# Gate products of a product-key expert layer from bf16 one-hots, the gate in three parts, the masks with four tokens innermost

## What is computed

```python
def block(xb):                       # 128 tokens
    q = (xb @ w_pq).reshape(PEER_BLOCK, P_HEADS, 2, P_HALF)
    sc = jnp.einsum('thpc,hpkc->thpk', q, sub_keys)
    sv, si = lax.top_k(sc, TOPK)
    cand = (sv[..., 0, :, None] + sv[..., 1, None, :])...     # 16 x 16 sums
    cid = (si[..., 0, :, None] * N_KEYS + si[..., 1, None, :])...
    fv, fi = lax.top_k(cand, TOPK)
    eid = jnp.take_along_axis(cid, fi, axis=-1)
    g = jax.nn.softmax(fv.astype(jnp.float32), axis=-1).astype(xb.dtype)
    ue = jnp.take(u_experts, eid, axis=0)
    ve = jnp.take(v_experts, eid, axis=0)
    a = jax.nn.gelu(jnp.einsum('thkd,td->thk', ue, xb), approximate=False)
    return jnp.einsum('thk,thkd->td', g * a, ve)
```

## Time and profile before

| | us |
|---|---|
| median of 3 runs (2201.74 to 2204.07) | 2202.97 |
| the profiled execution | 2208.66 |
| its span (first to last instruction) | 2207.0 |

### The profile page before, as it was taken

One profiled execution on the slowest core, in us unless ns is written; L12 is line 12 of the kernel. 1 busy time (PEld: TensorE's weight loads), 2 busy tenths in 40 slices (PEclk: granted clock), 3 DMA queues, 4 the chain that ended last, 5 costly groups with the idle time before them and its releaser, 6 DMA issues. The chain is left out here.

```text
span 2207.0 us, 46403 instructions
## 1 busy us (share of the span) xinstructions
PE 2152.3 (98%) x14712; PEld 2005.6 (91%) x14712; DVE 1683.5 (76%) x2461; ACT 1098.2 (50%) x1651; POOL 367.5 (17%) x344
## 2 busy tenths in 40 slices
PE   6999999999999999999989999999999999999998
PEld 6999899999999988888889989999999998888886
DVE  6665658999999687677775746599999996667776
ACT  6445454444444454554464545444444445554454
POOL 3110110000000155334230101100000002333442
PEclk9999999999999999999998999999999999999999
DMA  5444466765555677777644444567655557777774
GB/s 192 153 144 152 145 207 213 230 203 178 173 174 176 224 260 242 239 242 243 223 135 135 150 166 168 188 225 231 194 175 176 171 176 256 244 240 242 241 240 164
DMA packets 173982, 437.49 MB, mean 198 GB/s; under 512 B 19360, under 2 KB 84896, under 8 KB 172752
## 3 DMA queue, kind: packets, MB, share of 16 engines
q1 hardware_dynamic: 173232, 432.09, 59.5%
q0 software_dynamic: 672, 4.39, 0.6%
HBM read 399.70 MB, written 36.70 MB: 198 GB/s over the span
## 5 line engine op out<-in xcount | busy, mean ns | idle before, releaser
L746 DVE TENSOR_TENSOR w_lo<-raw,w_hi 128x1024 fp32r<-128x1024 f32 x680 | 844.7, 1245 | 401.8 <-ACT w_hi L714 183.1
L1143 PE MATMUL ps<-act_hi,w_hi 128*128 128x256 f32 x2880 | 829.6, 288 | 3.2 <-DVE act_lo L797 1.9
L1143 PE MATMUL ps<-act_lo,w_hi 128*128 128x256 f32 x2880 | 819.8, 285 | 0.0
L1143 PE MATMUL ps<-act_hi,w_lo 128*128 128x256 f32 x2880 | 819.8, 285 | 0.0
L1143 PEld LDWEIGHTS ps<-act_hi,w_hi 128*128 128x128 f32 x2880 | 558.1, 194 | 5.5 <-DVE act_lo L797 2.3
L1143 PEld LDWEIGHTS ps<-act_hi,w_lo 128*128 128x128 f32 x2880 | 558.2, 194 | 0.1
L1143 PEld LDWEIGHTS ps<-act_lo,w_hi 128*128 128x128 f32 x2880 | 557.5, 194 | 0.0
L714 ACT ACTIVATE w_hi<-raw 128x1024 fp32r<-128x1024 f32 x248 | 263.1, 1061 | 323.5 <-PE ps L1403 311.7
L1403 PE MATMUL ps<-w_hi,act_hi 128*128 128x512 f32 x1000 | 389.2, 389 | 2.0 <-DVE act_lo L1107 2.0
L1403 PE MATMUL ps<-w_lo,act_hi 128*128 128x512 f32 x1000 | 389.0, 389 | 0.0
L1403 PE MATMUL ps<-w_hi,act_lo 128*128 128x512 f32 x1000 | 389.0, 389 | 0.0
(11 more groups left out here) (248 smaller groups left out, 2105.9 us busy)
## 6 DMA issues: line engine op xcount, KB each, us to landing
raw<-slabs SPq DMA_DIRECT2D x684, 512.0 KB, 3.6
h_park<-h_out SPq DMA_DIRECT2D x256, 128.0 KB, 1.7
h_in<-h_park SPq DMA_DIRECT2D x250, 128.0 KB, 3.7
memT<-mem POOLq DMA_DIRECT2D x2, 1024.0 KB, 6.6
skT<-sub_keys POOLq DMA_DIRECT2D x2, 1024.0 KB, 8.0
x_park<-xT SPq DMA_DIRECT2D x2, 1024.0 KB, 5.4
xT<-x_park SPq DMA_DIRECT2D x2, 1024.0 KB, 8.4
xT<-x SPq DMA_DIRECT2D x1, 1024.0 KB, 5.0
```

The lines of the kernel that those rows point to most:

```text
L746: nc.vector.tensor_tensor(w_lo[:, j].rearrange("p k c -> p (k c)"), raw[:, j, :], w_hi[:, j].rearrange("p k c -> p (k c)").bitcast(FP32), ...
L1143: last = nc.tensor.matmul(ps[:, j, 0:T], w[:, j, k, :], a[:, k, :], start=(k == 0 and i == 0), stop=(k == KB - 1 and i == 2))
```

## The change

`iota`, `row_is` and the picks become bf16 (keys up to 127 are exact in it). `iota` and `row_is` get four tokens as their innermost dimension: `iota` holds each number four times in a row. `rowT`, `colT` and `gate2` become one tile `picks` with five rows: row key, column key, and the gate in three bf16 parts (rounded part, rounded rest, rest of the rest; `g_rest` is float32). `hot_row` becomes bf16, three parts, four tokens innermost; `hot_col` becomes bf16, still token by token in memory, but written through a view with the token innermost. The gate product has three matmuls a token for two, each reading `hot_row` with a step of four elements.

```diff
+PARTS = 3
-        hot_col = at("hot_col", x_at, [P, 4, P], F32R)
-        hot_row = at("hot_row", x_at + 2048, [P, 2, 4, P], F32R)
+        hot_col = at("hot_col", x_at, [P, 4, P], BF16)
+        hot_row = at("hot_row", x_at + 2048, [P, PARTS, P, 4], BF16)
-        iota = sb("iota", [P, P])
+        iota = at("iota", top[0], [P, P, 4], BF16)
-        row_is = at("row_is", par_at, [P, 4, P], BF16)
+        row_is = at("row_is", par_at, [P, P, 4], BF16)
-        rowT = sb("rowT", [P, T])
-        colT = sb("colT", [P, T])
-        gate2 = sb("gate2", [P, 2, T], F32R)
+        picks = at("picks", top[0], [P, 2 + PARTS, T], BF16)
+        g_rest = tmp("g_rest", 104, [P, T])
-            nc.gpsimd.iota(iota[:], [[1, P]], base=0, channel_multiplier=0,
+            nc.gpsimd.iota(iota[:], [[1, P], [0, 4]], base=0, channel_multiplier=0,
-                                                        (b_f, iota, ALU.is_equal, cols, col_f)):
+                                                        (b_f, iota[:, :, 0], ALU.is_equal, cols, col_f)):
-                step.mark(nc.vector.tensor_copy(rowT[:], ps[:, 4, 0:T]))
-                step.mark(nc.vector.tensor_copy(colT[:], ps[:, 4, T:2 * T]))
-                step.link(nc.vector.tensor_copy(gate2[:, 0], ps[:, 5, 0:T]))
-                step.link(nc.vector.tensor_tensor(gate2[:, 1], ps[:, 5, 0:T], gate2[:, 0].bitcast(FP32), ALU.subtract))
+                step.mark(nc.vector.tensor_copy(picks[:, 0:2], ps[:, 4, :].rearrange("p (i t) -> p i t", i=2)))
+                step.link(nc.vector.tensor_copy(picks[:, 2], ps[:, 5, 0:T]))
+                step.link(nc.vector.tensor_tensor(g_rest[:], ps[:, 5, 0:T], picks[:, 2], ALU.subtract))
+                step.link(nc.vector.tensor_copy(picks[:, 3], g_rest[:]))
+                step.link(nc.vector.tensor_tensor(picks[:, 4], g_rest[:], picks[:, 3], ALU.subtract))
-                    nc.vector.tensor_tensor(row_is[:], iota[:].unsqueeze(1).to_broadcast([P, 4, P]),
-                                            rowT[:, ds(n * 4, 4)].unsqueeze(2).to_broadcast([P, 4, P]),
+                    nc.vector.tensor_tensor(row_is[:], iota[:],
+                                            picks[:, 0, ds(n * 4, 4)].unsqueeze(1).to_broadcast([P, P, 4]),
-                    nc.vector.tensor_tensor(hot_col[:], iota[:].unsqueeze(1).to_broadcast([P, 4, P]),
-                                            colT[:, ds(n * 4, 4)].unsqueeze(2).to_broadcast([P, 4, P]),
+                    nc.vector.tensor_tensor(hot_col[:].rearrange("p t c -> p c t"), iota[:],
+                                            picks[:, 1, ds(n * 4, 4)].unsqueeze(1).to_broadcast([P, P, 4]),
-                    nc.vector.tensor_tensor(hot_row[:], row_is[:].unsqueeze(1).to_broadcast([P, 2, 4, P]),
-                                            gate2[:, :, ds(n * 4, 4)].bitcast(FP32).unsqueeze(3).to_broadcast([P, 2, 4, P]),
+                    nc.vector.tensor_tensor(hot_row[:], row_is[:].unsqueeze(1).to_broadcast([P, PARTS, P, 4]),
+                                            picks[:, 2:2 + PARTS, ds(n * 4, 4)].unsqueeze(2).to_broadcast([P, PARTS, P, 4]),
-                        for part in range(2):
+                        for part in range(PARTS):
                             last = nc.tensor.matmul(ps[:, 4 + s, i * P:(i + 1) * P], hot_col[:, i, :],
-                                                    hot_row[:, part, i, :], start=(part == 0), stop=(part == 1))
+                                                    hot_row[:, part, :, i], start=(part == 0), stop=(part == PARTS - 1))
```

More of the change, by code:

```diff
@@ L176, in trunk @@
         tri = sb("tri", [P, P])
-        iota = sb("iota", [P, P])
+        iota = at("iota", top[0], [P, P, 4], BF16)
+        top[0] += P * 4 * 2
         cand_at = sb("cand_at", [P, TOPK])
@@ L182, in trunk @@
         wif_lo = sb("wif_lo", [P, KB, 8], F32R)
-        row_is = at("row_is", par_at, [P, 4, P], BF16)
+        row_is = at("row_is", par_at, [P, P, 4], BF16)
         assert top[0] - par_at >= 4 * P * 2
-        rowT = sb("rowT", [P, T])
-        colT = sb("colT", [P, T])
-        gate2 = sb("gate2", [P, 2, T], F32R)
+        picks = at("picks", top[0], [P, 2 + PARTS, T], BF16)
+        top[0] += (2 + PARTS) * T * 2
         gated_at = top[0]
```

## The result

The changed kernel takes 2386.62 us (median of 4 runs), the kernel before 2203.52 beside it: a ratio of 1.083, with a 95% interval from 1.0804 to 1.0856. I had forecast 2192.7, with a range up to 2232. The change costs 183 us.

What follows compares the result with a forecast made beforehand. TensorE and VectorE were taken to bound the gate stretches equally at 3.77 us a group, with TensorE leading afterwards. 128 x -0.082 = -10.5, set-up +0.2, gives -10.3: from 2202.97 to 2192.7 us, range 2176 to 2232.

Steps and rivals of the forecast that it cites:

- What bounds the kernel: Gate stretches, 128 groups: TensorE and VectorE both need 3.77 us a group, and the group takes the longer.
- TensorE, the pace of the gate matmuls: Gate product: 12 bf16 matmuls at 64 ns each, 0.77 us against 0.85, -0.08 us a group.
- I take it as free: Gate matmuls' moving operand: reading with a step of four elements (8 bytes) was taken to cost nothing.
- loads still pace: Rival, gate matmuls: weight loads no faster or stepped read as dear, 0.106 us each, +0.42 a group, 2257 us; chance 0.18.
- VectorE, double speed: row_is and hot_row on 16-bit data at 0.52 ns an element, each 0.27 us less, to 0.61 and 0.87.
- VectorE, hot_col: hot_col's write with a step of 128 elements stays at one element a time, 0.61 us start to start.
- The rival: hot_col's hopping writes at 2.5 ns an element add 0.74 us, VectorE leads at 3.96, 2227 us; chance 0.22.
- The loop: hot_col waits for the previous gate matmuls (one buffer); next one-hots ready at about 2.6 of 3.69 us, so not limiting.
- Small edits: Set-up about 2.3 us for 1.67, costing 0.1 to 0.2 in all; stepped iota comparison free; longer iota at start covered.

Runs made afterwards that it cites:

- e1: The changed kernel with hot_col written in the order of its memory (ones and zeros in wrong places): 2264.5 us.
- e2: The changed kernel with each gate matmul reading 128 neighbouring elements of hot_row instead of every fourth (wrong elements): 2356.8 us.
- e3: The changed kernel with hot_col written in memory order and the gate matmuls reading hot_row in order (gates wrong): 2185.3 us.
- e5: The changed kernel with rows of hot_col 512 bytes apart instead of 256: 2388.1 us.
- e4: The kernel before with hot_col, still float32r, written token innermost, each four-byte element hopping 512 bytes: 2241.3 us.
- e10: The changed kernel with pairs of tokens innermost in hot_col, row_is and hot_row, written in memory order, read 4 bytes apart, results correct: 2185.1 us, ratio 0.9911.
- e12: The changed kernel with hot_col holding pairs of tokens innermost, written in runs of two elements with a hop after each: 2269.9 us.

## Why the prediction was wrong

- **What bounds the kernel** was read rightly: both engines need the same time, and the group takes the longer. The later groups bear it out: 4.27 us in e1, 4.96 in e2 and 3.61 in e3 gave 2264.5, 2356.8 and 2185.3 us, where 2205 + 128 x (group - 3.77) says 2269, 2357 and 2185. Only where hop and step stand together (the changed kernel and e5, 5.18) does the loop make the group longer than either engine's own need.
- **TensorE, the pace of the gate matmuls** was the first step that failed. I had taken 64 ns; it was 108. The step that was wrong is the one sentence "I take it as free" on the moving read. The weight loads, on which I had put the whole doubt, don't set it: with the read in order the pace is 55 ns (e2, e3), near the low bound of 53 that I had set for the columns alone. The rule on fast loads (the Trainium skill, TensorE: Matmul & The Clock Gate, Weight-path perf modes) is borne out by the records of the loads, 98 ns for bf16 (e2, e3) against 192 for float32r; the 81 ns of the same page's Back-to-back issue gap is not, since 55 was measured. The rival "loads still pace" gave the right number (106) for the wrong reason, and I had written "or the stepped read costs as much" into it without weighing it by itself. The 8-byte step deserved a rival of its own. This step alone puts the time outside the range: e1 has it without the hop, and took 2264.5.
- **VectorE, double speed** was right for row_is (0.42 us) and, once the hop is out of its way, for hot_row (0.95 us, e1), both as worked out; in the changed kernel hot_row took 1.18.
- **VectorE, hot_col** was the second and larger failure: "it stays at one element a time, 0.61" against a start-to-start of 2.12 us. The rival had the mechanism and the place right and the size wrong by a factor of 2.5: it priced the growth at 0.74 us from act_lo's 2.5 ns an element, a row of four-byte writes that don't hop, and the growth was 1.8 (2.51 for 0.69). The figures of the Trainium skill that I put beside it (Vector Engine (DVE) Microarchitecture Reference, Measured stream behaviour on trn2) stand there for streams of four-byte words, where e4 bears them out; I carried them over to two bytes without a word on that.
- **The loop,** which "stays open" by the prediction, was worked out from both numbers, and its slack fell with them. With 2.12 us for hot_col, and 1.30 for the starts of the gate matmuls in place of 0.77, the loop leads at 5.18.
- **The range** ended at 2232, and so left out a price that the prediction itself had: the stepped read in full, 2257. With the hop at the rival's 2.5 ns beside it that would not have been more, since the one covers the other (4.19 us a group for TensorE, 3.96 for VectorE). Beyond that goes only the true size of the hop (e2, which has it alone, took 2356.8): the dearest price seen in a trace is not a bound for a form that the trace doesn't have.
- **Small edits.** The stepped iota at L1050 took 2.29 us against 2.28: free, as taken. The set-up took 2.39 us (490.52 to 492.91) against about 2.3 worked out. For the first one-hots of a layer TensorE waited 2.06 us in the first and 1.45 in the second, where 1.1 to 1.2 in the second alone was forecast: hot_col came late there too. With the hop gone hardly any of it is left (0.4 us in all, in e10). The iota at the start grew from 0.24 to 1.19 us under the cover that I had named.
- **Where the gain would have been.** Without hop and step the forecast had the right direction and was some 10 us too cautious: the group is 3.61 us (e3) for my 3.69, since 12 matmuls start within 0.66 us and not 0.77. e10 reaches that (3.62) with every gate in its place.

## What to carry to other kernels

An edit that puts a small dimension innermost to speed up one engine must be priced on every reader and writer of the tile: here it made two VectorE instructions faster, and the same view made the third 3.6 times as long and every gate matmul twice as long as it need be. Write down for each access how many bytes lie side by side and how far the next run is; for two-byte data keep at least a whole four-byte word together on each side. Where a form of access is nowhere in the trace, give it a rival of its own, with a price well beyond the dearest row, or measure it by a one-line edit that puts the elements in the wrong place: e1, e2 and e3 did just that and explained the whole loss.

## What the runs showed of the hardware that I had not expected

- VectorE, writes that hop at each element: 1.8 to 1.9 ns for a four-byte word (e4, e12), 4.6 ns for two bytes (changed kernel, e5), the same at 256 and 512 bytes. Behind the two-byte form the next instruction is 0.23 us longer (1.18 for 0.95); behind the four-byte form it isn't.
- TensorE, a bf16 moving operand of 128 columns: 55 ns a matmul in order, 56 with a step of 4 bytes, 108 with 8 bytes. bf16 weights with a step of 8 bytes stay hidden under it (57 ns).
- bf16 matmuls with a weight load each reach 55 ns at 128 columns, where float32r ones take 106. Three bf16 matmuls are cheaper than two float32r ones at this width: 0.165 us for 0.21.
- VectorE's two-source instructions on 16-bit data run two elements at a time also where the innermost run is two elements long and one operand is repeated (0.55 us for 768 elements, e10).
- Short one-source instructions on 128 elements cost 0.175 us with one scalar from SBUF and 0.22 with two, from one start to the next.
